# Token rows of each stage at an offset of their own within 128 bytes

## The reference

```python
def swiglu(x, w_gu, w_down):
    gate, up = jnp.split(x @ w_gu, 2, axis=-1)
    return (jax.nn.silu(gate) * up) @ w_down
```

## Time and profile before

| | before |
|---|---|
| median of three runs (range) | 1196.7 us (1196.52 to 1197.67) |
| span of the profiled execution | 1195.0 us |
| median less that span | 1.7 us |
| TensorE matmul busy | 1187.3 us, 99% |
| TensorE weight load busy | 1089.4 us, 91% |
| VectorE busy | 934.7 us, 78% |
| ScalarE busy | 730.4 us, 61% |
| GpSimd busy | 77.9 us, 7% |
| moved by DMA | 209.92 MB, 176 GB/s on average |
| chain that ended last | TensorE 93%, VectorE 4%, the rest 3% |

### The profile page before, as it was taken

One profiled execution on the slowest core, in us unless ns is written; L12 is line 12 of the kernel. 1 busy time (PEld: TensorE's weight loads), 2 busy tenths in 40 slices (PEclk: granted clock), 3 DMA queues, 4 the chain that ended last, 5 costly groups with the idle time before them and its releaser, 6 DMA issues.

```text
span 1195.0 us, 22393 instructions
## 1 busy us (share of the span) xinstructions
PE 1187.3 (99%) x7956; PEld 1089.4 (91%) x7956; DVE 934.7 (78%) x1617; ACT 730.4 (61%) x1211; POOL 77.9 (7%) x91
## 2 busy tenths in 40 slices
PE   9999999999999999999999999999999999999998
PEld 9899999888888999999888889988888989888887
DVE  7766788988876788688988767888876787888853
ACT  7564746666654588567666645666664567666642
POOL 4460000000000000610000000000000000000000
PEclk9999999999999999999999999999999999999999
DMA  8545655554654445115555743655663423555730
GB/s 329 184 142 187 232 189 177 186 208 176 230 214 154 141 170 188 41 36 177 211 178 204 258 151 123 211 176 194 219 239 135 150 91 125 195 205 178 255 131 36
DMA packets 48143, 209.92 MB, mean 176 GB/s; under 512 B 3486, under 2 KB 4908, under 8 KB 43596
## 3 DMA queue, kind: packets, MB, share of 16 engines
q1 hardware_dynamic: 46720, 204.96, 48.7%
q10 hardware_dynamic: 1356, 4.07, 1.0%
HBM read 207.90 MB, written 1.13 MB: 175 GB/s over the span
## 4 chain that ended last, share of the span: by engine, by line
PE 93%; DVE 4%; ACT 1%; issue 1%; DMA 1%; DVEq 0%; SPq 0%; ACTq 0%
PE main L2165 25%; PE main L2167 13%; PE main L2523 13%; PE main L2138 8%; PE main L2139 8%; PE main L2140 8%; PE main L2525 7%; DVE w_lo L1157 1%; PE side L2303 1%; PE main L2566 1%; PE side L2566 1%; PE side L2277 1%; PE main L2682 1%; PE main L2854 1%; PE main L2858 1%
## 5 line engine op out<-in xcount | busy, mean ns | idle before, releaser
L1157 DVE TENSOR_TENSOR w_lo<-raw,w_hi 128x1024 fp32r<-128x1024 f32 (+3 forms) x365 | 466.8, 1287 | 5.0 <-ACT w_hi L594 3.8
L2165 PE MATMUL main<-xs,w_hi 128*128 128x512 f32 x1328 | 461.3, 390 | 0.2 <-DVE xs L1191 0.2
L594 ACT ACTIVATE w_hi<-raw 128x1024 fp32r<-128x1024 f32 (+2 forms) x363 | 402.5, 1111 | 68.3 <-PE main L2140 53.0
L2167 PE MATMUL main<-xs,w_lo 128*128 128x256 f32 x1328 | 374.5, 282 | 0.0
L2165 PEld LDWEIGHTS main<-xs,w_hi 128*128 128x128 f32 x1328 | 249.2, 188 | 53.2 <-DVE w_lo L1157 0.7
L2167 PEld LDWEIGHTS main<-xs,w_lo 128*128 128x128 f32 x1328 | 251.0, 189 | 0.0
L2523 PE MATMUL main<-h_both,w_hi 128*128 128x512 f32 x682 | 236.6, 390 | 0.0
L2525 PE MATMUL main<-h_both,w_lo 128*128 128x256 f32 x682 | 192.3, 282 | 0.0
L2523 PEld LDWEIGHTS main<-h_both,w_hi 128*128 128x128 f32 x682 | 128.0, 188 | 26.8
L2525 PEld LDWEIGHTS main<-h_both,w_lo 128*128 128x128 f32 x682 | 128.9, 189 | 0.0
L2138 PE MATMUL main<-xs,w_hi 128*128 128x256 f32 x368 | 105.4, 286 | 0.0
(11 more groups left out here) (505 smaller groups left out, 1869.6 us busy)
## 6 DMA issues: line engine op xcount, KB each, us to landing
raw<-in_w_gu_a SPq DMA_DIRECT2D x44, 1024.0 KB, 5.2
raw<-in_w_gu_b SPq DMA_DIRECT2D x44, 1024.0 KB, 5.2
raw<-in_w_down_a SPq DMA_DIRECT2D x16, 1408.0 KB, 6.1
raw<-in_w_down_b SPq DMA_DIRECT2D x16, 1408.0 KB, 6.0
raw<-in_w_in SPq DMA_DIRECT2D x15, 1024.0 KB, 5.4
raw<-in_w_in_a SPq DMA_DIRECT2D x13, 1024.0 KB, 5.2
raw<-in_w_gates SPq DMA_DIRECT2D x4, 1024.0 KB, 5.1
raw<-in_w_up SPq DMA_DIRECT2D x4, 1024.0 KB, 5.2
```

Of the source, the lines that this page charges most:

```text
L594: act.activation(w_hi[:, u % RING, 0:n], raw[:, s % RAW, u % 2, 0:n], ACT.Copy).then_inc(hi_ready, 1)
L1157: return dve.tensor_tensor(dst, src, hi.bitcast(F32), ALU.subtract)
L2165: pe.matmul(bank[:, :], piece(w_hi, u, k), xs[:, k], start=k == 0, stop=k == KC - 1, skip_group_check=True)
L2167: ins = pe.matmul(bank[:, 0:SEQ], piece(w_lo, u, k), xs_hi[:, k], start=False, stop=k == KC - 1, skip_group_check=True)
```

## The change

`xs` becomes seven tensors, one for each stage, at the end of `x` plus an offset of `XS_AT`, and `h_both` four, at its old place plus an offset of `H_AT`. Since the end of `x` is at a multiple of 128 and the old place of `h_both` at 32, the moving rows begin within 128 bytes at 96, 80, 112, 96, 112, 72 and 40 in the projections and at 48, 72, 80 and 16 in the down stages. `xg` moves 48 bytes down, so its rows begin at 48 and their last 256 tokens at 112. The helper `placed` allocates a tensor from the multiple of 32 below and returns the part that begins at the wanted byte. The tensors of different stages overlap, as the one tensor did before. What lies behind `h_both` moves up by 96 bytes, from 32 to 0 within 128 bytes: `gate_n`, `gate_s`, `hid`, `xk_hi`, `xk_lo`, `k_nope`, `k_rope`, `v_mla`, `v_pad_b` and `final`. Every operation is the same as before, with the stage's tensor in the place of the common one.

```diff
@@ -54,6 +54,10 @@
 UNIT = 11 * P
 
 
+XS_AT = {"out1": 96, "ffn_a1": 80, "mix_a": 112, "ffn_a2": 96, "ffn_b1": 112, "mix_b": 72, "ffn_b2": 40}
+H_AT = {"a1": 16, "a2": 40, "b1": 48, "b2": 112}
+
+
 def first_unit(name):
     return 2 * FIRST_SLAB[name]
 
@@ -163,11 +167,20 @@
             return (nc.alloc_sbuf_tensor_at(name, list(shape), dtype, offset=at),
                     (at + int(np.prod(shape[1:])) * 4 + 31) // 32 * 32)
 
+        def placed(name, at, n):
+
+            e = at % 32 // 4
+            return nc.alloc_sbuf_tensor_at(name, [P, e + n], F32R, offset=at - 4 * e)[:, e:e + n]
+
         x, at = place("x", (nc.sbuf_base + 31) // 32 * 32, [P, KC, SEQ])
-        xs, _ = place("xs", at + 32, [P, KC, 2, SEQ], F32R)
-        xs_hi, xs_lo = xs[:, :, 0], xs[:, :, 1]
+        xs_of = {name: placed("xs_" + name, at + off, KC * 2 * SEQ).rearrange("p (k i n) -> p k i n", k=KC, i=2)
+                 for name, off in XS_AT.items()}
+        xs_hi_of = {name: v[:, :, 0] for name, v in xs_of.items()}
+        xs_lo_of = {name: v[:, :, 1] for name, v in xs_of.items()}
         at_raw = at + 4 * 2 * KC * TOK
-        xg, at = place("xg", at_raw - 32 - 4 * 2 * KC * X_ROW, [P, 2, KC, X_ROW], F32R)
+        xg = placed("xg", at_raw - 80 - 4 * 2 * KC * X_ROW, 2 * KC * X_ROW)\
+            .rearrange("p (i k n) -> p i k n", i=2, k=KC)
+        at = at_raw
         xg_hi, xg_lo = xg[:, 0, :, 0:TOK], xg[:, 1, :, 0:TOK]
         assert at <= at_raw
         raw, at = place("raw", at_raw, [P, RAW, 2, UNIT])
@@ -190,8 +203,9 @@
         free0 = at
 
 
-        h_both, at = place("h_both", free0, [P, 2, FT, SEQ], F32R)
-        h_hi, h_lo = h_both[:, 0], h_both[:, 1]
+        h_of = {name: placed("h_" + name, free0 + off, 2 * FT * SEQ).rearrange("p (i k n) -> p i k n", i=2, k=FT)
+                for name, off in H_AT.items()}
+        at = free0 + 4 * 2 * FT * SEQ + 96
         mix_end = at
         gate_n, at = place("gate_n", at, [P, 2, SEQ])
         gate_s, at = place("gate_s", at, [P, 2, SEQ])
...
@@ -821,7 +836,7 @@
-                    act.activation(h_hi[:, row, :], hid[:, t % 2, :], ACT.Copy).then_inc(h_hi_ready, 1)
+                    act.activation(h_of[which][:, 0, row, :], hid[:, t % 2, :], ACT.Copy).then_inc(h_hi_ready, 1)
...
@@ -1492,7 +1507,7 @@
-                    scale_lo(xs_lo[:, row, :], xm, gain(split, row), xs_hi[:, row, :],
+                    scale_lo(xs_lo_of[split][:, row, :], xm, gain(split, row), xs_hi_of[split][:, row, :],
...
@@ -1550,7 +1565,7 @@
-                    low(h_lo[:, tt, :], hid[:, t % 2, :], h_hi[:, tt, :]).then_inc(h_ready, 1)
+                    low(h_of[which][:, 1, tt, :], hid[:, t % 2, :], h_of[which][:, 0, tt, :]).then_inc(h_ready, 1)
...
@@ -2156,7 +2171,7 @@
-            def project_halves(u, bank, off=0, first=None):
+            def project_halves(u, bank, xs, off=0, first=None):
...
@@ -2489,17 +2504,18 @@
+                xs, h_both = xs_of[FFN_NORM[which]], h_of[which]
-                        enter(u0, [bank_of(t0 + j) for j in range(2)], (xs_hi, xs_lo) if which == "b2" else (xs,), first,
+                        enter(u0, [bank_of(t0 + j) for j in range(2)], (xs[:, :, 0], xs[:, :, 1]) if which == "b2" else (xs,), first,
-                            project(u0 + j, bank_of(t0 + j)[:, 0:SEQ], xs_hi, xs_lo,
+                            project(u0 + j, bank_of(t0 + j)[:, 0:SEQ], xs[:, :, 0], xs[:, :, 1],
-                            project_halves(u0 + j, bank_of(t0 + j, i * 4), i * 4, first if j == 0 else None)
+                            project_halves(u0 + j, bank_of(t0 + j, i * 4), xs, i * 4, first if j == 0 else None)
...
@@ -2522,11 +2538,11 @@
-                                ins = pe.matmul(bank[:, 0:SEQ], piece(w_lo, u, b), h_hi[:, k, :], start=False,
+                                ins = pe.matmul(bank[:, 0:SEQ], piece(w_lo, u, b), h_both[:, 0, k, :], start=False,
-                                             h_hi[:, k, :], h_lo[:, k, :], k == 0, k == FT - 1)
+                                             h_both[:, 0, k, :], h_both[:, 1, k, :], k == 0, k == FT - 1)
...
```

More of the change, by code:

```diff
@@ L769, in _ @@
                     act.wait_ge(x_new, k + 1)
-                    scale_hi(xs_hi[:, k, :], x[:, k, :], gain("ffn_a1", k))
+                    scale_hi(xs_hi_of["ffn_a1"][:, k, :], x[:, k, :], gain("ffn_a1", k))
                     square_free(SQ0["ffn_a1"] + k)
@@ L782, in residual @@
                 if name != "end2":
-                    scale_hi(xs_hi[:, row, :], x[:, row, :], gain("ffn_b1" if name == "kv" else name, row))
+                    split = "ffn_b1" if name == "kv" else name
+                    scale_hi(xs_hi_of[split][:, row, :], x[:, row, :], gain(split, row))
                 square(x[:, row, :], SEQ, c + m)
@@ L1118, in row_hi @@
                 act.wait_ge(evac, FIRST_TILE["out_b"] + m // 2 + 1)
-                scale_hi(xs_hi[:, m, :], x[:, m, :], gain("ffn_b2", m))
+                scale_hi(xs_hi_of["ffn_b2"][:, m, :], x[:, m, :], gain("ffn_b2", m))
             def pair_square(j):
@@ L1422, in _ @@
                 dve.wait_ge(merged_hi, m + 1)
-                low(xs_lo[:, m, :], merged[:, m % 2, :], xs_hi[:, m, :]).then_inc(merged_split, 1)
+                low(xs_lo_of["out1"][:, m, :], merged[:, m % 2, :], xs_hi_of["out1"][:, m, :]).then_inc(merged_split, 1)
             slot(first_unit("w_up") + KC - 1)
@@ L1846, in _ @@
                 dve.wait_ge(h_hi_ready, f * FT + t + 1)
-                low(h_lo[:, t, :], hid[:, t, :], h_hi[:, t, :]).then_inc(h_ready, 1)
+                low(h_of["b1"][:, 1, t, :], hid[:, t, :], h_of["b1"][:, 0, t, :]).then_inc(h_ready, 1)
                 if t == 0:
@@ L2166, in project_halves @@
                               skip_group_check=True)
-                    ins = pe.matmul(bank[:, 0:SEQ], piece(w_lo, u, k), xs_hi[:, k], start=False, stop=k == KC - 1,
+                    ins = pe.matmul(bank[:, 0:SEQ], piece(w_lo, u, k), xs[:, k, 0], start=False, stop=k == KC - 1,
                                     skip_group_check=True)
@@ L2576, in first_level @@
                 ins.then_inc(joined, 1)
-            enter(u0, [bank_of(in_tile(t)) for t in range(2)], (xs_hi, xs_lo), XG0["mix_a"], norm="mix_a")
+            enter(u0, [bank_of(in_tile(t)) for t in range(2)], (xs_hi_of["mix_a"], xs_lo_of["mix_a"]), XG0["mix_a"], norm="mix_a")
             for t in range(2, 24):
-                project(u0 + t, bank_of(in_tile(t))[:, 0:SEQ], xs_hi, xs_lo)
+                project(u0 + t, bank_of(in_tile(t))[:, 0:SEQ], xs_hi_of["mix_a"], xs_lo_of["mix_a"])
                 if t == 2:
@@ L2822, in _ @@
             t0, u0 = FIRST_TILE["in_b"], first_unit("w_in_b")
[L2823 removed]
+            enter(u0, [bank_of(t0 + j) for j in range(2)], (xs_hi_of["mix_b"], xs_lo_of["mix_b"]), XG0["mix_b"], norm="mix_b")
             for j in range(2, 4):
[L2825 removed]
+                project(u0 + j, bank_of(t0 + j)[:, 0:SEQ], xs_hi_of["mix_b"], xs_lo_of["mix_b"])
             pe.wait_ge(qsq_ready, 2)
```

22 lines of the change are left out of this document (10 added, 12 removed).

## The result

The changed kernel takes 1205.35 us (1205.33 to 1206.03, three runs) against 1196.7 before: 8.65 us or 0.7% slower, a ratio of 1.0071 with a 95% interval of 1.0053 to 1.0089. The profiled execution is the one of 1205.35, with a span of 1203.6, so 1.75 us lie around the span here too. The prediction said 1192.6, and a range that ended at 1199.5.

What follows compares the result with a forecast made beforehand. The prediction took TensorE's matmul pace as the bound. Pairs -3.9, triples -0.3 and kv copies +0.1 us summed to -4.1 us, taking the median from 1196.7 to 1192.6 us, range 1186 to 1199.5.

Steps and rivals of the forecast that it cites:

- The bound: Whole kernel: TensorE busy 1187.3 of 1195.0 us, so an edit helps or hurts only through the pace of its matmuls.
- ScalarE and VectorE at 0.0 us: Their writes of the same rows at other offsets: any slowdown is covered beside TensorE, so a cost of 0.0 us.
- The pairs: 512- plus 256-column matmuls in projections and down stages: 2.3 ns faster wherever the residue modulo 64 changes, 3.9 us gained.
- the one step that the trace shows twice: Loop slips from a slow into a fast pattern: 3.5 ns for three matmuls, 2.3 ns for the two of a pair.
- The period of 64 bytes: Offsets equal modulo 64 behave alike, so ffn_a2's projections, 336 pairs going from 32 to 96, keep their pace.
- The bounds: Limits for a pair, from 346.8 ns: 340.0 ns, 13.6 us gained, to 351.6 ns, 9.7 us lost.
- The triples: Three 256-column matmuls: 96 in ffn_b1's first projections, mix_b and ffn_b2's entry fall into the fast pace, 0.3 us gained.
- The shifted kv copies: 24 triples over xk, rows now at 0: 355 ns instead of about 351, 0.1 us lost.
- Rival 4: 32 was the good residue; every other costs 2 ns a matmul, in pairs and triples: 1207.9 us, chance 0.11.
- Rival 1: The offset does not matter: all residues give 346.8 ns a pair, time 1196.7 us, chance 0.27.
- Rival 3: Rows starting 8 past a multiple of 16 (stages at 40 and 72) cost 2.2 ns a matmul: 1199.3 us, chance 0.09.

Runs made afterwards that it cites:

- The map: Paces by row offset, weights at 0, from the earlier and changed kernels and further ones with other row offsets; three built for it took 1213.0, 1214.5 and 1211.1 us.

## Why the prediction was wrong, point by point

- *The bound.* Right. Everything hung on the pace of the matmuls, nothing on waits, transfers or the other engines' writes.
- *ScalarE and VectorE at 0.0 us.* Right: their busy times are the same to 0.7 us.
- *The pairs.* This is the step that failed, in the words of the prediction: "I take the one step that the trace shows twice", "I give the step to every pair whose residue changes modulo 64". The size of a step was sound in kind (3.33 ns instead of 2.3). Its sign was a guess. I read the 118.3 ns of the pair's short matmul as the slow triple's, so as a slow pattern that any other offset could only leave. The map shows that for pairs over weights at 0 this is the fast pattern: of the 21 other offsets read none is below 346.7, and sixteen are above. Instead of -3.9 us the pairs cost +8.6.
- *The period of 64 bytes.* Wrong. a2's projections went from 346.7 to 350.1 between 32 and 96, and the down stages at 16 and 80 differ by 6.7 ns. A period of 16, 32 or 64 bytes does not fit the map. Whether 128 is one was not tested.
- *The bounds.* 351.6 ns above was too low; 359.7 was reached at 72. It came from rows over another kind of operand, with one offset of its own. The 340.0 below came out to the digit, and that was luck. It was built on 116.7 ns for the short matmul of the fast triple, but over other weights that matmul takes 113.3 (a triple of 340.0), and by the same sum the bound would have been 333.3. In the pairs of 340.0 the 512 columns take 226.8 and the 256 columns 113.3 ns, not 223.4 and 116.7. It took the weights' offset to reach it, which this change does not touch. No single pair in any of the traces took less than 339 ns.
- *The triples.* The 0.3 us were looked for in small stages. There the triples went from 352.0 to 345.0 at 112, from 351.5 to 361.9 at 72 and from 353.3 to 359.2 at 40, so they lost 0.3. The mixer's triples gained 1.5 us of pace, and VectorE beside them let through 0.2. The prediction had treated the cover only the other way round, as what hides a slower ScalarE or VectorE, and asked by average busy shares whether a faster TensorE would meet a wait. In the mixer the chain, not the share, would have told.
- *The shifted kv copies.* Right: their triples went from 351.6 to 355.7 ns, the 0.1 us that was put down.
- *Rival 4* ("32 was the good residue", 1207.9, a chance of 0.11) is nearest to what happened, 2.6 us over the measured time. That its number came so near is partly luck: it charged 2 ns for every matmul at every other residue, while pairs at 16 and 40 cost nothing and those at 72 cost 13 ns. Its two witnesses, 272 columns at 96 and weights as moving rows at 0, had been set aside as foreign cases. Rival 1 falls with the result. Rival 3 is right for 72 (+13 ns) and wrong for 40 (0), and the starts inside a group of 16 bytes do not order the map: offsets of 12 and 28 are as fast as 16 and 32, and 0 and 64 are slow. The Trainium skill ("SBUF — State Buffer", Specifications) states 16-byte cachelines and a penalty for each cross to a new line; the map of pairs shows no such order.

The forecast also gave a gain more weight than the evidence had. The trace held one offset; of the two foreign ones in it, both were slower.

## What to carry to other kernels

When TensorE is bound by its own pace, the distance between starts, not the busy share, is what to read, and the addresses of the moving rows and of the weights within 128 bytes moved it between 340.0 and 360.0 ns for a pair, 6%. Choose them together, for each form of loop, by one run in which every stage has another row offset and every ring slot another weight offset, and read the last pairs of a slot, after the loop has settled. Then run the choice several times, since a good combination can still fall into a second pattern. A stage whose TensorE is level with VectorE did not pay out a faster pace here.

## What the runs showed of the hardware that was not expected

- Loops of fp32r matmuls settle into short patterns that repeat for hundreds of loops in a row. The mean of most of them is 340.0, 346.7, 350.0, 353.3, 356.7 or 360.0 ns for 768 columns. The best, 340.0, is 20 ns over the 320 ns of the columns at 2.4 GHz, for pairs and for triples alike, and it goes with the columns: 226.8 ns for 512 and 113.3 for 256.
- Which pace it is depends on the offsets of the moving rows, of w_hi and of w_lo together, down to 4 bytes (16: 346.7, 20: 355.6, 24: 360.0), and for triples also on something in the tensor itself (rows at 112: 343 over `xs`, 351.5 over `xg`).
- Some combinations hold two patterns: rows at 32 over weights at 0 gave triples of 350.0 or 353.5, rows at 80 gave pairs of 350.0 to 350.2 or 353.3, rows at 16 over w_lo at 32 pairs of 340.1 or 346.7.
- What in the memory or in TensorE makes the loops lock in was not settled. That the load of the next weights and the stream of rows get into each other's way would fit all of this, but no run took the loads away, and it is only argued.
